# Taps right after their evacuation, weight splits ahead of it, and the residual scaled early: a reordered projection stage in a two-block fp32 kernel

## The chip, the cores and the metric

The program runs on one core of one Trainium2 chip. The metric is the device time of one execution in microseconds. The engines are TensorE (PE, the matrix multiplier), VectorE (DVE), ScalarE (ACT) and GpSimd (POOL); SyncE (SP), ACT and POOL also issue DMAs. Each engine works through its own instructions in order, and semaphores tie the engines together.

## The reference

Two transformer blocks on a sequence of 512 tokens with 1024 channels, in fp32. The first block (spatial gating, forgetting attention, a convolutional feed-forward net) is untouched by the change. Between the blocks stands a normalisation, and the second block starts from its result:

```python
    x = first_block(...)            # ends with: return rms_norm(x, norm_final_g)
    return second_block(x, ...)

def second_block(x, ...):
        h = rmsnorm(x, norm_gain[l])
        proj = jnp.einsum('btd,dc->btc', h, w_in[l])
        (dn_q, dn_k, dn_v, dn_z, dn_b, dn_a, df_q, df_k, df_v, df_z) = jnp.split(proj, ...)
        o_dn = gated_deltanet_group(...)
        o_df = diff_attention_group(...)
        x = x + jnp.einsum('btc,cd->btd', concat([o_dn, o_df]), w_out[l])

def gated_deltanet_group(q, k, v, z, bb, aa, conv_w, a_log, dt_bias, out_gain):
    qkv = silu(causal_depthwise_conv(concat([q, k, v]), conv_w))     # 4 taps
    q = l2norm(q) * DN_HEAD_K ** -0.5;  k = l2norm(k)
    beta = sigmoid(bb);  g = -exp(a_log) * softplus(aa + dt_bias)
    o = gated_delta_rule(q, k, v, g, beta)
    ...
```

## The kernel before

Activations lie channel-major in SBUF: X is 8 tiles (KC) of 128 channels x 512 tokens. Every fp32 product is made from three products of split numbers: a high part (GH for activations, HI for weights) and a low remainder (GL, LO). The function `product` makes one output tile of 128 channels from 8 x 3 matmuls of 128x512.

Weights arrive as a stream of units of 128x1024 in a ring of four slots. For each unit SP loads RAW and POOL loads HI (the same bytes, of which HI keeps the high part) as soon as `unit_done` says that the unit four places earlier is used up. DVE then makes LO = RAW - HI: that is `ring_low`, written as `("ring", unit)` in the order tables. A product waits for its unit's split (`unit_split`).

The stage in question is the first of the second block. It multiplies by the gates' unit (`ba`: beta and decay, 36 rows) and by twelve units `kqv` 0 to 11 (four tiles each of keys, queries, values of the delta rule, written to KT, QT, VT). For each tile t:

- PE makes the product in one of two banks (`bank_of`), and may start it when the tile two earlier has been evacuated (`gemm_freed`).
- DVE evacuates it times the token factor RB into CB (`evacuate`, L1509).
- ACT makes the last tap, CB times a weight (L1308).
- DVE adds three taps, each waiting for the one before it (L1894).
- ACT applies silu (L1315) and, for keys and queries, squares (L1320) into SQ2; PE sums the squares per token (`l2s`, L650). After four tiles ACT takes roots and DVE reciprocals (`l2r`), PE spreads them over the partitions (`l2b`, L656), and DVE multiplies (L1913).

Around these stand the gates' rows (`rows`: softplus, cumulative sums, exponentials, on ACT and DVE in turns), `lam` and `scalars` (the factor of differential attention), `egb` (rows reread from HBM), `cols` (the rows turned to columns), and `spill`, which writes X to HBM, as its place in SBUF is reused. At the kernel's end XR reads it back, DVE multiplies it by the final norm's gain and by R1B (the norm's token factor, spread over the partitions by PE into PS[6] and copied by ACT, L1312), and adds the last product.

After the twelve tiles PE goes on with `dfv` (values of differential attention), which waits for the evacuation of tile 11, and with `GK` 0, the Gram product of the keys, which waits for the last normalised key tile (`l2_made` 4, from `l2b` 3 on DVE).

What sets the order is written out by hand: all engines walk the same list, MIX2_ORDER, and each picks out what it has to do. `_projections` writes this stage's list and `_ring` puts the splits into it.

## Time and profile before

| | us |
|---|---|
| median of 3 runs | 984.22 (979.09 to 984.84) |
| the profiled execution | 979.09 |
| its span, first to last instruction | 977.4 |
| PE busy | 937.8 (96%) |
| DVE busy | 565.4 (58%) |
| ACT busy | 303.5 (31%) |
| mean granted clock of PE | 0.987 |

The time of the profiled execution is 1.7 us longer than its span, and it was the fastest of the three runs. PE is busy nearly throughout, so what counts is where it waits. The projection stage lies between about 590 and 677 us from the span's start.

### The profile page before, as it was taken

To read this page: it belongs to the slowest core of one execution; us is meant where nothing else is said; L and a number is where in the kernel's file an instruction comes from. 1 tells how busy PE (TensorE), PEld (TensorE's weight loads), DVE (VectorE), ACT (ScalarE), POOL (GpSimd) and SP (SyncE) were. 2 spreads that over 40 slices of the span, in tenths; PEclk is the share of its full clock that TensorE was granted. 3 is DMA by queue.
4 is the path that set the end of the run, shared out by engine and by line. 5 is a ranking of instruction groups with operands and counts; after the bars stand their busy time and mean duration, and the time that the engine had idled before them with its cause. 6 is when DMAs were issued, how large, how long until landed. Compare 5 with 4: busy or idle time off the path is not lost.

```text
span 977.4 us, 13547 instructions
## 1 busy us (share of the span) xinstructions
PE 937.8 (96%) x4666; PEld 762.6 (78%) x4666; DVE 565.4 (58%) x968; ACT 303.5 (31%) x609; POOL 72.3 (7%) x138
## 2 busy tenths in 40 slices
PE   9997998999999999999999999999999887889998
PEld 7886776788888888888888888888879774667777
DVE  6265446364877767776434336868563647625454
ACT  6143465433322222222101115434112234432410
POOL 0100000010110101010101000000000000000000
PEclk9998999999999999999999999999999989999999
DMA  8755332255656565656565655665353121113354
GB/s 275 228 187 193 129 130 88 87 177 179 204 185 202 183 203 183 204 181 205 179 205 178 200 186 166 218 210 166 105 161 120 45 86 44 44 44 108 110 187 156
DMA packets 49614, 154.84 MB, mean 158 GB/s; under 512 B 9488, under 2 KB 10512, under 8 KB 49312
## 3 DMA queue, kind: packets, MB, share of 16 engines
q1 hardware_dynamic: 22176, 75.70, 24.2%
q0 software_dynamic: 19008, 69.21, 21.7%
q10 hardware_dynamic: 8384, 9.29, 2.9%
q8 instruction: 31, 0.51, 0.2%
q14 instruction: 15, 0.12, 0.0%
HBM read 149.70 MB, written 4.49 MB: 158 GB/s over the span
## 4 chain that ended last, share of the span: by engine, by line
PE 85%; DVE 6%; ACT 3%; issue 3%; DMA 3%; ACTq 0%; DVEq 0%; SPq 0%; POOLq 0%
PE bank L593 70%; DMA HI<-wstream 2%; PE bank L650 2%; PE bank L1015 1%; PE bank L752 1%; PE bank L728 1%; PE bank L656 1%; PE bank L983 1%; PE bank L977 1%; PE bank L963 1%; PE bank L922 1%; PE bank L930 1%; PE bank L742 1%; DVE bank L1855 1%; PE bank L940 1%
## 5 line engine op out<-in xcount | busy, mean ns | idle before, releaser
L593 PE MATMUL bank<-GH,HI 128*128 128x512 f32 x720 | 290.1, 403 | 2.1 <-ACT DV L1355 1.4
L593 PE MATMUL bank<-GH,LO 128*128 128x512 f32 x720 | 282.4, 392 | 0.0
L593 PE MATMUL bank<-GL,HI 128*128 128x512 f32 x720 | 282.0, 392 | 0.0
L1517 DVE TENSOR_TENSOR LO<-RAW,HI 128x1024 fp32r<-128x1024 f32 x88 | 107.7, 1224 | 121.6 <-DMA HI<-wstream 120.7
L593 PEld LDWEIGHTS bank<-GH,HI 128*128 128x128 f32 x720 | 136.3, 189 | 31.3 <-issue 2.8
L593 PEld LDWEIGHTS bank<-GH,LO 128*128 128x128 f32 x720 | 135.9, 189 | 29.1
L593 PEld LDWEIGHTS bank<-GL,HI 128*128 128x128 f32 x720 | 136.3, 189 | 25.4
L575 POOL DMA_DIRECT2D HI<-wstream x132 | 69.8, 529 | 880.5 <-PE bank L593 871.5
L1238 ACT ACTIVATE YC<-AB,PAR 128x512 f32<-128x512 f32 x44 | 36.0, 818 | 140.5 <-DVE AB L1664 140.5
L593 PE MATMUL bank<-AH,HI 128*128 128x512 f32 x176 | 69.4, 394 | 0.0
L593 PE MATMUL bank<-AH,LO 128*128 128x512 f32 x176 | 69.0, 392 | 0.0
L593 PE MATMUL bank<-AL,HI 128*128 128x512 f32 x176 | 68.4, 388 | 0.0
L1664 DVE TENSOR_TENSOR AB<-bank,RB 128x512 f32<-128x512 f32 x44 | 30.4, 691 | 48.5 <-PE bank L593 48.5
L1658 DVE TENSOR_TENSOR LO<-RAW,HI 128x1024 fp32r<-128x1024 f32 x44 | 53.6, 1219 | 3.6 <-DMA HI<-wstream 3.6
L593 PEld LDWEIGHTS bank<-AH,LO 128*128 128x128 f32 x176 | 33.0, 188 | 7.7
L593 PE MATMUL bank<-HI,GH 128*128 128x512 f32 x96 | 38.4, 400 | 0.5 <-DVE LO L1524 0.5
L593 PEld LDWEIGHTS bank<-AL,HI 128*128 128x128 f32 x176 | 33.0, 188 | 7.3
L1126 ACT ACTIVATE GH<-X,SM 128x512 fp32r<-128x512 f32 x8 | 5.8, 725 | 104.7 <-DVE X L1722 104.7
L593 PEld LDWEIGHTS bank<-AH,HI 128*128 128x128 f32 x176 | 33.1, 188 | 6.6
L593 PE MATMUL bank<-LO,GH 128*128 128x512 f32 x96 | 37.5, 390 | 0.0
L593 PE MATMUL bank<-HI,GL 128*128 128x512 f32 x96 | 37.4, 390 | 0.0
L1675 DVE SCALAR_TENSOR_TENSOR YC<-AB,PAR,YC 128x512 f32<-128x512 f32 x44 | 33.1, 752 | 6.0 <-DVE YC L1671 0.3
(289 smaller groups left out, 1264.0 us busy)
## 6 DMA issues: line engine op xcount, KB each, us to landing
RAW<-wstream SPq DMA_DIRECT2D x135, 512.0 KB, 3.8
HI<-wstream POOLq DMA_DIRECT2D x132, 512.0 KB, 4.9
X<-x_t SPq DMA_DIRECT2D x8, 256.0 KB, 7.7
NCB<-out_t ACTq DMA_DIRECT2D x1, 2048.0 KB, 10.2
out_t<-X ACTq DMA_DIRECT2D x8, 256.0 KB, 5.2
XR<-out_t ACTq DMA_DIRECT2D x8, 256.0 KB, 3.6
out_t<-XR SPq DMA_DIRECT2D x8, 256.0 KB, 2.6
EG<-out_t ACTq DMA_DIRECT2D x1, 1024.0 KB, 4.9
```

The costliest lines, as they stand in the source:

```text
L575: pool.dma_start(HI[:, s, :], wstream[bass.ds(2 * i + s // 2, 1), :, 1024 * (s % 2):1024 * (s % 2 + 1)] .rearrange("o p n -> p (o n)")).th ...
L593: mm = pe.matmul(out, a, b, start=(first and n == 0), stop=(last and n == 2))
L650: mm = pe.matmul(out[:, n * b:n * (b + 1)], src[:, P * b:P * (b + 1)], groups, start=True, stop=True)
L656: mm = pe.matmul(out[:, P * b:P * (b + 1)], column(b), IDENT, start=True, stop=True)
L728: pe.matmul(PS[2 + e][:, 0:w], q[r, 4 + p, P * i:P * (i + 1)], k[r, p, 0:w], start=(part == 0), stop=False)
L742: mm = pe.transpose(PS[4 + e][:, P * j:P * (j + 1)], P1[:, 2 * (n % 2) + e, P * j:P * (j + 1)], IDENT)
L752: mm = pe.matmul(PS[6][64 * e:64 * e + 64, P * j:T], VB[:, j, P * p + 64 * e:P * p + 64 * (e + 1)], PT1[:, e, j, P * j:T], start=(j == 0), ...
L1238: act.activation(YC[:, gv, :], AB[:, gv, 2:T + 2], ACT.Identity, scale=PAR[:, bass.ds(6 * t + (C_FCW + 3 * gv + 2), 1)], bias=PAR[:, bass. ...
L1517: dve.tensor_tensor(LO[:, u % RING, :], RAW[:, u % RING, :], HI[:, u % RING, :].bitcast(F32), ALU.subtract).then_inc(unit_split, 1)
L1658: dve.tensor_tensor(LO[:, slot, :], RAW[:, slot, :], HI[:, slot, :].bitcast(F32), ALU.subtract).then_inc(unit_split, 1)
L1664: dve.tensor_tensor(AB[:, gv, 2:T + 2], up_bank(G_UP + 2 * tt + gv)[:, :], RB[:, :], ALU.mult)\
L1675: dve.scalar_tensor_tensor(YC[:, gv, :], AB[:, gv, 0:T], PAR[:, bass.ds(6 * t + (C_FCW + 3 * gv), 1)], YC[:, gv, :], ALU.mult, ALU.add).th ...
```

## The change

The change has five parts. (1) Each tile's taps, silu and square come right after its evacuation in the list, instead of behind the other work of its round. (2) The split of the unit three ahead (`ring`) comes before the evacuation of a tile, not after it. (3) The gates' rows, `egb`, `scalars` and `cols` are moved later, behind tiles whose taps are now complete. (4) X is multiplied by gain and token factor in place, straight from PS[6], in four steps (`x2`, 8 DVE instructions) behind tiles 7 to 10, and is written to HBM after that; so R1B, ACT's copy into it and the 8 multiplications at the kernel's end go, and `dfv` 0 waits for the eight updates. (5) In the first round PE makes tile 0's products with k = 2 to 6 before the last product of the gates' unit. Besides, the sums of squares of tiles 4 to 7 go to the same bank as those of 0 to 3.

```diff
 def _projections():
-    order = [("ba", 0), ("rows", 0)]
+    order = [("ba", 0)]
     for t in range(12):
         if t in (6, 10):
             order.append(("l2r", t // 4 - 1))
         order.append(("kqv", t))
+        if t == 5:
+            order.append(("scalars", 0))
+        if t in (0, 2):
+            order.append(("rows", t // 2))
         if t == 0:
-            order += [("lam", 0), ("rows", 1)]
-        if t == 2:
+            order.append(("lam", 0))
+        if t == 4:
             order.append(("egb", 0))
-        if t == 3:
-            order.append(("scalars", 0))
-        if t == 5:
+        if 7 <= t <= 10:
+            order.append(("x2", t - 7))
+        if t == 6:
             order.append(("cols", 0))
-        if 4 <= t <= 7:
-            order.append(("spill", t - 4))
         if 2 <= t <= 9:
             order.append(("l2s", t - 2))
         if t >= 8:
             order.append(("l2b", t - 8))
-        order.append(("taps", t))
...
 def _ring(order):
     for what, n in order:
+        if what == "kqv" and n:
+            out.append(("ring", U_KQV + n + RING - 1))
         out.append((what, n))
-        if what == "kqv":
-            out.append(("ring", U_KQV + n + RING - 1))
...
+        elif what == "ba":
+            out.append(("ring", U_KQV + RING - 1))
...
             def head_sums(t):
                 pe.wait_ge(l2_sq, t + 1)
-                token_sums(PS[5 + 2 * (t // 4)][:, NB * t:NB * (t + 1)], SQ2[:, t % 2, :]).then_inc(l2_mm, 1)
+                if t == 4:
+                    pe.wait_ge(l2_rt, 1)
+                token_sums(PS[5][:, NB * t:NB * (t + 1)], SQ2[:, t % 2, :]).then_inc(l2_mm, 1)
...
+                    product(U_KQV, G_KQV, gl_made, 2 * KC, ks=range(2, KC - 1))
                     product(U_BA, G_BA, gl_made, 2 * KC, ks=(KC - 1,))
-                    product(U_KQV, G_KQV, gl_made, 2 * KC, ks=range(2, KC))
+                    product(U_KQV, G_KQV, gl_made, 2 * KC, ks=(KC - 1,))
...
                     if n == 0:
                         pe.wait_ge(gemm_freed, G_DFQK)
                         pe.wait_ge(rb_ready, 3)
-                        pe.wait_ge(r1_kept, 1)
+                        pe.wait_ge(x_updated, KC)
...
                     act.activation(tile_of(n), CB[:, n % 2, 3:T + 3], ACT.Copy,
                                    scale=par(C_DCW + 4 * n + 3)).then_inc(cv_a, 1)
-                    if n == 0:
-                        act.wait_ge(r1_mm, 1)
-                        act.activation(R1B[:, :], PS[6][:, :], ACT.Copy).then_inc(r1_kept, 1)
-                elif what == "taps":
                     act.wait_ge(cv_v, n + 1)
                     act.activation(tile_of(n), tile_of(n), ACT.Silu).then_inc(cv_s, 1)
...
-                elif what == "spill":
+                elif what == "x2":
                     if n == 0:
                         act.wait_ge(scratch_landed, LANDED_ROWS)
                     for k in (2 * n, 2 * n + 1):
                         if k < KC - 1:
+                            act.wait_ge(x_updated, k + 1)
                             act.dma_start(out_t[P * k:P * (k + 1), :], X[:, k, :]).then_inc(x_spilled, 16)
...
                 elif what == "kqv":
                     evacuate(G_KQV + n, U_KQV + n, CB[:, n % 2, 3:T + 3])
-                elif what == "taps":
                     dve.wait_ge(cv_a, n + 1)
...
+                elif what == "x2":
+                    dve.wait_ge(r1_mm, 1)
+                    for k in (2 * n, 2 * n + 1):
+                        dve.scalar_tensor_tensor(X[:, k, :], X[:, k, :], par(C_GFIN + k), PS[6][:, :],
+                                                 ALU.mult, ALU.mult).then_inc(x_updated, 1)
...
             for m in range(KC):
                 dve.wait_ge(x_landed[m], 32)
-                then(dve.scalar_tensor_tensor(XR[:, m, :], XR[:, m, :], par(C_GFIN + m), R1B[:, :], ALU.mult, ALU.mult))
                 dve.wait_ge(unit_done, U_WO2 + m + 1)
```

Two engines show how the order moves. DVE at the start of the stage, from the evacuation of the gates' product (BR) on; CB is the evacuated tile, LO the split, KT the taps, R_.. and RS the gates' rows. Before:

```order
L1509 TENSOR_TENSOR BR<-bank,RB 36x512
L1886 MEMSET CB 128x2x3
L1748 TENSOR_SCALAR R_99<-BR,PAR 4x512
L1749 MEMSET RS 128x512
L1509 TENSOR_TENSOR CB<-bank,RB 128x512
L1517 TENSOR_TENSOR LO<-RAW,HI 128x1024
L1753 TENSOR_SCALAR R_99<-R_99 4x512
L1754 TENSOR_TENSOR R_99<-R_99,R_100 4x512
L1755 TENSOR_SCALAR R_99<-R_99,SM 4x512
L1757 SCALAR_TENSOR_TENSOR RS<-CON,R_99 4x64 x8
L1762 TENSOR_TENSOR R_99<-RS 4x512
L1894 SCALAR_TENSOR_TENSOR KT<-CB,PAR,KT 128x512 x3
```

Now, in the changed kernel (its own line numbers):

```order
L1513 TENSOR_TENSOR BR<-bank,RB 36x512
L1890 MEMSET CB 128x2x3
L1521 TENSOR_TENSOR LO<-RAW,HI 128x1024
L1513 TENSOR_TENSOR CB<-bank,RB 128x512
L1897 SCALAR_TENSOR_TENSOR KT<-CB,PAR,KT 128x512 x3
L1752 TENSOR_SCALAR R_98<-BR,PAR 4x512
L1753 MEMSET RS 128x512
L1521 TENSOR_TENSOR LO<-RAW,HI 128x1024
L1513 TENSOR_TENSOR CB<-bank,RB 128x512
L1897 SCALAR_TENSOR_TENSOR KT<-CB,PAR,KT 128x512 x3
```

The split moved ahead of the evacuation, and the taps follow it at once; the rows' sums (L1753 to L1762 before) moved behind tile 2.

ACT at the same place, from its copy of the token factor RB on. Before:

```order
L1274 ACTIVATE RB<-bank 128x512
L1280 ACT_TABLE_LOAD
L1280 ACTIVATE SM<-PAR 4x1
L1282 ACTIVATE R_100<-R_99 4x512
L1284 ACTIVATE R_100<-R_100 4x512
L1286 ACT_TABLE_LOAD
L1286 ACTIVATE R_100<-R_100,SM 4x512
L1308 ACTIVATE KT<-CB,PAR 128x512
L1312 ACTIVATE R1B<-bank 128x512
L1303 ACT_TABLE_LOAD
L1303 ACTIVATE SM<-bank 128x2
```

Now:

```order
L1279 ACTIVATE RB<-bank 128x512
L1313 ACTIVATE KT<-CB,PAR 128x512
L1316 ACT_TABLE_LOAD
L1316 ACTIVATE KT<-KT 128x512
L1321 ACTIVATE SQ_101<-KT 128x512
L1285 ACT_TABLE_LOAD
L1285 ACTIVATE SM<-PAR 4x1
L1287 ACTIVATE R_99<-R_98 4x512
L1289 ACTIVATE R_99<-R_99 4x512
L1291 ACT_TABLE_LOAD
L1291 ACTIVATE R_99<-R_99,SM 4x512
L1308 ACT_TABLE_LOAD
L1308 ACTIVATE SM<-bank 128x2
L1313 ACTIVATE KT<-CB,PAR 128x512
```

The gates' softplus (L1280 to L1286 before) and the exponential of `lam` (L1303 before), with their three table loads, moved from ahead of tile 0's copy to between tile 0's square and tile 1's copy.

## Rows read from the trace of the kernel before

**Rows 1.** Page, part 4: the chain that ended last, by engine
```profile
PE 85%; DVE 6%; ACT 3%; issue 3%; DMA 3%; ACTq 0%; DVEq 0%; SPq 0%; POOLq 0%
```

**Rows 2.** Windows: busy us of PE, PEld, DVE, ACT, POOL; granted clock; DMA
```profile
590.00:700.00 110.00, 109.05 (x585) 93.44 (x584) 76.71 (x120) 44.30 (x61) 8.44 (x16) 1.00 0.56 177
```

**Rows 3.** Timeline of PE: start us, us, instruction, [idle before it, releaser]
```profile
612.81 1.05 PE L650 MATMUL bank<-CON,SQ 128*128 128x1 f32 x8 [0.68 <-ACT SQ L1320]
...
676.22 1.05 PE L886 MATMUL bank<-KT 128*128 128x128 f32 x8
```

**Rows 4.** Timeline of DVE, first tile: split, rows, taps, next evacuation
```profile
602.62 1.23 DVE L1517 TENSOR_TENSOR LO<-RAW,HI 128x1024 fp32r<-128x1024 f32 x1
604.89 0.42 DVE L1753 TENSOR_SCALAR R<-R 4x512 f32<-4x512 f32 x1 [1.05 <-ACT R L1286]
...
608.76 2.30 DVE L1894 SCALAR_TENSOR_TENSOR KT<-CB,PAR,KT 128x512 f32<-128x512 f32 x3
```

**Rows 5.** Timeline of ACT, same stretch
```profile
600.09 1.28 ACT L1280 ACT_TABLE_LOAD   x1
...
602.85 1.28 ACT L1286 ACT_TABLE_LOAD   x1
...
604.77 0.70 ACT L1308 ACTIVATE KT<-CB,PAR 128x512 f32<-128x512 f32 x1
...
607.26 0.17 ACT L1303 ACTIVATE SM<-bank 128x2 f32<-128x2 f32 x1
...
612.13 0.63 ACT L1320 ACTIVATE SQ<-KT 128x512 f32<-128x512 f32 x1
```

**Rows 6.** Timeline of DVE, tile 8: evacuation, split, normalisation, taps
```profile
651.69 0.69 DVE L1509 TENSOR_TENSOR CB<-bank,RB 128x512 f32<-128x512 f32 x1 [2.15 <-PE bank L593]
652.42 1.23 DVE L1517 TENSOR_TENSOR LO<-RAW,HI 128x1024 fp32r<-128x1024 f32 x1
653.56 0.68 DVE L1913 TENSOR_TENSOR KT<-KT,bank 128x512 f32<-128x512 f32 x1
654.16 2.33 DVE L1894 SCALAR_TENSOR_TENSOR VT<-CB,PAR,VT 128x512 f32<-128x512 f32 x3
```

**Rows 7.** Timeline of ACT, tile 8: the copy
```profile
652.42 0.72 ACT L1308 ACTIVATE VT<-CB,PAR 128x512 f32<-128x512 f32 x1 [1.55 <-DVE CB L1509]
```

**Rows 8.** Timeline of DVE: cols, the reciprocal of l2r, two multiplies from a bank
```profile
634.20 0.48 DVE L1901 MEMSET ST<- 128x512 f32 x1
...
635.38 2.32 DVE L1894 SCALAR_TENSOR_TENSOR QT<-CB,PAR,QT 128x512 f32<-128x512 f32 x3
...
640.65 0.25 DVE L1910 RECIPROCAL SM<-SM 128x16 f32<-128x16 f32 x1 [2.94 <-ACT SM L1360]
...
934.02 1.40 DVE L1974 SCALAR_TENSOR_TENSOR QT<-bank,PAR,ZT 128x512 f32<-128x512 f32 x2
```

**Rows 9.** The chain in order of time: start us, us, engine, line, count
```profile
613.86 5.61 PE bank L593 x24
```

**Rows 10.** HI loads: one issue on POOL, and time to landing, 585 to 680
```profile
595.07 0.53 POOL L575 DMA_DIRECT2D HI<-wstream  x1 [8.13 <-PE bank L593]
...
DMA to landing us min/median/max: 4.5/5.4/6.3
```

**Rows 11.** Windows around three waits of PE: columns as in rows 2
```profile
84.00:90.00 6.00, 0.85 (x5) 0.39 (x3) 5.50 (x14) 2.49 (x5) 0.00 (x0) 0.94 0.36 116
90.00:96.00 6.00, 6.00 (x19) 4.81 (x20) 1.04 (x5) 2.43 (x10) 0.00 (x0) 0.50 0.00 0
...
724.00:727.00 3.00, 1.33 (x11) 0.92 (x9) 0.00 (x0) 0.63 (x1) 0.54 (x1) 1.00 0.88 198
727.00:731.00 4.00, 4.00 (x26) 3.49 (x24) 2.48 (x6) 1.09 (x2) 0.00 (x0) 1.00 0.26 93
```

**Rows 12.** Timeline of DVE at the kernel's end
```profile
969.42 0.75 DVE L1989 SCALAR_TENSOR_TENSOR XR<-XR,PAR,R1B 128x512 f32<-128x512 f32 x1
974.26 0.69 DVE L1991 TENSOR_TENSOR XR<-XR,bank 128x512 f32<-128x512 f32 x1 [4.09 <-PE bank L593]
```

8 lines of the change are left out of this document (4 added, 4 removed).

## The prediction, made before the changed kernel ran

> **What bounds the kernel now.** I read the chain that ended last first: PE holds 85% of it [rows 1], so a change can only pay, or cost, where PE waits. Then the windows of the projection stage: of 110 us PE is busy 109.05, DVE 76.71 and ACT 44.30, at a granted clock of 1.00 [rows 2]. So 0.95 us is all that any reordering can win there. The timeline of PE shows 0.68 of it as one wait, for the squares of tile 0 [rows 3]. DVE looks free for a third of the time, but the sums say nothing about how its waits are spread: the reader should see in the timelines of DVE and ACT what stands between one tile's taps and the next one's, and how it was hidden. Before the change, DVE used the time of ACT's copy for a split (evacuation 651.69, split 652.42, taps 654.16; ACT's copy of 0.72 ran beside the split) [rows 6, 7], and the rows' softplus on ACT ran beside the product and the split of tile 0, before any tap was due [rows 4, 5].
>
> **The change, part by part.** The marker is the start of Gram product 0, which in the trace begins at 676.22 [rows 3]. It needs the last normalised key tile, which is last in DVE's order of this stage, so it shows when DVE and ACT are through. I follow their chain in the new order.
>
> Start of the chain. The split of unit `kqv` 3 now stands ahead of the evacuation of tile 0. Its load may start when the gates' unit is used up, and that is now 15 matmuls later. A tile's 24 matmuls take 5.6 us [rows 9], so these are 3.4 to 3.5. The load's issue goes from 595.07 to about 598.5, and it lands 5.4 (median) to 6.3 us later [rows 10]: 603.9 to 604.8. The next load is issued under 1 us behind it, so I take 604.2. Before, the same split ran at 602.62 without a wait [rows 4]. DVE waits some 3 us here with nothing else to do, and the evacuation, the copy and everything after stand behind it.
>
> One round of DVE. Split 1.14 (652.42 to 653.56), evacuation 0.73 (651.69 to 652.42), ACT's copy 0.72 plus a step of 0.03, three taps 2.25 (2.33 less the overlap with the next instruction) [rows 6, 7]. Together 4.87. The copy's 0.75 is new on this path: the split that hid it stands before the evacuation now. Tile 0's taps end at 604.2 + 4.87 = 609.1.
>
> The detour on ACT. ACT now does tile 0's silu and square (0.63 each), then the softplus and `lam`, then tile 1's copy. From the rows: one table load and three activations 2.76 (600.09 to 602.85), a load and the logarithm 1.92 (to 604.77), a load of 1.28 with the exponential of 0.17, the copy 0.70 [rows 5]. With the two of 0.63 that is 8.1 us, in which DVE's taps of tile 1 wait: until 617.2. They end at 619.4. This is the work that used to be hidden, and its cover is gone because a tile's taps now stand on both sides of it.
>
> The rest. Ten more rounds (tiles 2 to 11) are 48.7. Between them stand on DVE: the rows' sums 3.87 (604.89 to 608.76) [rows 4]; `cols` 1.18; `x2` 8 instructions at 1.40 a pair, 5.6 [rows 8]; four multiplications of `l2b` at 0.60, 2.4 [rows 6]; `l2r` 0, for which DVE waits until ACT has done silu, square, a table load and the root, 0.63 + 0.63 + 1.28 + 0.3, and then 0.2 for itself, 3.1; `l2r` 1 the same but with `x2` and `l2b` beside it (2.0 us), while ACT also waits for the updates and issues two writes of X, some 1.7. Sum 17.8. The chain ends at 619.4 + 48.7 + 17.8 = 685.9, against 676.22: **9.7 us later**. With the landing at 603.8 it is 9.3, at 604.8 it is 10.3.
>
> Is PE ahead of it all the time? Yes by its own pace: a tile is 5.6 us [rows 9] and the sums about 0.8 between (1.05 with its overlap) [rows 3], so after 0.68 us less at tile 0 PE would reach Gram product 0 at 675.3. It is then held where its waits look: by the squares of tile 1 (619.4 + 1.3 = 620.7, wanted at 618.5), 2 us; by the evacuation of tile 3, before tile 5, 2 us; by the first roots, 3 us, a wait that is new at the sums of tile 4, since both groups share a bank; by the evacuation of tile 11 before `dfv` 0, about 2 us, since its split and the last `x2` and `l2b` now stand ahead of it; and by the last key tile, 1 us. These are 10 us. The eight updates of X are done before tile 11's evacuation and hold nothing by themselves. The loads on SP and POOL follow `unit_done`, so they shift with PE, and have at least 0.5 us to spare against DVE after the first one, except near tile 7, where a landing of 6.3 instead of 5.4 would add 0.5.
>
> After the stage. The next chain (decays, Gram products, their gather and scatter through HBM) starts from PE's and DVE's last steps here, and so moves as a whole; I see nothing that gives time back. At the end of the kernel 8 instructions of 0.75 go, but DVE waits 4.09 us for PE behind the last of them [rows 12]: 0 us.
>
> The clock. A wait of about 5 us (84 to 90) was followed by six microseconds at 0.50, which is 1.2 GHz; one of 1.67 us (724 to 727) by 1.00 throughout [rows 11]. New waits of 2 to 3 us lie between. A fall costs half of its length in matmuls where PE sets the time. I count one, at the 3 us wait before tile 7: it bounds from 0 to 3 us, and I take 1.7, since the wait is nearer to the row of 1.67 than to that of 5.
>
> **Sum:** 9.7 + 1.7 = 11.4 us. On the profiled execution of 979.09 (span 977.4 and 1.7 around it) that is 990.5; on the median of 984.22 it is 995.6. The measured median should lie between, nearer to the second, as two of three runs lie near 984: **995**.
>
> ACT's table loads bear most on the detour. In the rows a load takes 1.28 and the whole step with the logarithm 1.92 [rows 5], 0.64 more, which is what an activation of this size takes (0.63): nothing else is paid for the switch. The Trainium skill, "ScalarE: Activation LUTs", section "What ACT_TABLE_LOAD costs", puts a drain of about 1380 ns beside a load of about 1283 ns; the load agrees with the trace, the drain does not show in it. By that page the five loads on the path would add an estimated 6.9 us more, and the sum would be 18.3.
>
> **The rivals.**
> 1. *The stage stays PE-bound.* If DVE, busy for 76.71 of 110 us, kept up, only the 0.95 us of idle would go: 984.2 - 0.9 = 983.3. For it speaks the sum of busy times [rows 2]; against it that twelve rounds of 4.87, 17.8 of inserts and the 8.1 us detour fill the stage without a gap. 0.12.
> 2. *Only the late waits hold.* The detour is absorbed and PE waits only before `dfv` 0 and Gram product 0, where the split stands ahead of tile 11's evacuation: 3 us less the 0.95: 986.3. It needs the first landing before 601 and a detour under 3 us; neither fits the rows. 0.11.
> 3. *The clock falls after three or four waits.* The waits at tiles 1, 5, 6 and before `dfv` 0 each cost up to 1.7, partly absorbed by the next wait: 9.7 + 5 = 14.7, or 998.9. The row of 0.50 speaks for it, the one of 1.67 us against. 0.12.
> 4. *The end was bound by DVE.* The 8 multiplications at 0.75 were on the path in the last 30 us: 6.0 and the 0.95 go, 977.3, faster than before. It decides if DVE is never waiting for PE there; the 4.09 us of waiting says that it is. 0.03.
> 5. *Each switch of tables costs its drain too*, as if ACT stood still after every load. Priced by the rows, as one more load of 1.28 at each of the five on the path [rows 5], it adds 6.4: 984.2 + 17.8 = 1002.0. The rows speak against it, since the logarithm is through 0.64 us after its load. This is the rule of the Trainium skill's page above, whose own figure gives 1002.5. 0.03.
>
> **How the numbers follow.** My forecast, 9 to 13 us more, has 0.59; the rivals have 0.12, 0.11, 0.12, 0.03 and 0.03. The range runs from the profiled execution's 979.09 plus 9.3 without a fall of the clock, 988.4, to 999 with the third rival; I put the lower end at 987.5. That leaves out rivals 1, 2, 4, 5 for the most part, some 0.2 to 0.25, and it is as wide as the unknown base (979 or 984) and the clock make it. One per cent, 9.8 us, is about what a measurement of this kernel can tell from no change. My bare chain of 9.3 to 10.3 lies on that line, and the clock pushes over it: four in five of the forecast, and rivals 3 and 5, are slower by more, 0.60; rivals 1 and 2 and the rest of the forecast are within, 0.36; faster 0.04.
>
> **What the next profile would show.** DVE waiting some 3 us for the HI load of the first split, near 601; taps of tile 1 starting near 617, not 613; DVE nearly without waits for PE until 685; PE waiting five times, on ACT's squares, on DVE's evacuations and on ACT's root, 10 us in all; Gram product 0 near 686; the tail's DVE rows shorter and the tail itself as long as before. The prediction is wrong if tile 1's copy on ACT comes before 614, if PE's waits sum to under 5 us, or if the distance from Gram product 0 to the end is not the 301 us that it was.

## The result, and the profile of the changed kernel

| | before | changed |
|---|---|---|
| median, us | 983.24 (979.09 to 984.84, 4 runs) | 993.37 (992.38 to 994.17, 4 runs) |
| ratio, 95% interval | | 1.0135, 1.0093 to 1.0177 |
| profiled execution, its span | 979.09, 977.4 | 996.08, 994.4 |
| end of ACT's copy of RB | 600.08 | 602.83 |
| start of Gram product 0 | 676.22 | 692.78 |
| from the first to the second: the stage | 76.14 | 89.95 |
| Gram product 0 to the end of the span | 301.18 | 301.62 |

The changed kernel is slower, by 9 to 17 us. The medians are those of four executions each; the ratio comes from more: 24 executions of the changed kernel, and from the experiments 70 of the kernel before, are on record. Their means are 995.9 and 983.3, 12.6 apart, give or take 1.7. (One execution of the kernel before and one of a_ba, over 1.5% above the fastest of their kernel, are left out of all means and ratios.)

In the profiled pair the spans differ by 17.0: 2.75 arose ahead of the stage, in code whose work the change doesn't touch, 13.8 in the stage, 0.4 behind it. The stage is measured from ACT's copy of the token factor RB, since nothing of it can be evacuated earlier; that takes the 2.75 out. Each stage below is that of one profiled execution. How much it varies between executions of one kernel is not on record, so what follows from a stage is held against the times of all executions further down.

PE's share of the chain that ended last, from part 4 of the page, answers to [rows 1]. DVE has taken most of what PE lost (6 to 10%); ACT, the DMAs and "issue" have one per cent more each:

```profile
PE 76%; DVE 10%; issue 4%; ACT 4%; DMA 4%; ACTq 0%; DVEq 0%; SPq 0%; POOLq 0%
```

The windows of the changed kernel, with the columns of [rows 2]. The first row is the same stretch of 110 us: PE is now idle for almost 10 us of it, and its mean clock is 0.95, not 1.00. The other two show where the clock was at 0.50, one of its two levels (1.2 GHz), for all or a part of the row:

```profile
590.00:700.00 110.00, 100.33 (x492) 83.97 (x491) 74.64 (x120) 47.49 (x64) 7.38 (x14) 0.95 0.50 166
625.00:630.00 5.00, 4.08 (x14) 3.60 (x15) 4.04 (x7) 2.06 (x4) 0.00 (x0) 0.50 0.45 163
651.00:655.00 4.00, 3.87 (x16) 3.27 (x17) 3.00 (x5) 1.93 (x2) 0.00 (x0) 0.67 0.44 155
```

What PE waited for in the stage of the changed kernel (waits: us in total, times, longest), 9.7 us. Before there were 0.95, of which 0.68 was one wait [rows 3]:

```profile
PE bank L652 <- ACT SQ L1321: 3.0, 1, 3.0
PE bank L652 <- ACT SM L1363: 2.7, 1, 2.7
PE bank L595 <- DVE CB L1513: 1.5, 1, 1.5
PE bank L595 <- DVE LO L1521: 1.4, 1, 1.4
PE bank L890 <- DVE KT L1922: 0.8, 1, 0.8
PE bank L595 <- issue: 0.3, 1, 0.3
```

They are, in this order, the squares of tile 1, the first roots, the evacuation of tile 11 ahead of `dfv` 0, the evacuation of tile 0 ahead of tile 2 (it ends right after DVE's split, which the profile names), and the last key tile ahead of Gram product 0. The sixth, 0.3, was there before.

The chain that ended last, in order of time, at the start of the stage. Each row is the piece that the next one had waited for, so it can be read as a list of what sets the time (a load on POOL's queue, the split, the evacuation of tile 0, ACT's copy, three taps, silu, square, then a detour over ACT, the copy of tile 1 and its taps):

```profile
601.26 7.59 DMA HI<-wstream
...
608.93 1.22 DVE LO L1521
610.15 0.61 DVE CB L1513
610.79 0.73 ACT KT L1313
...
611.62 0.76 DVE KT L1897
...
613.98 0.65 ACT KT L1316
614.64 0.64 ACT SQ L1321
615.29 1.28 ACT L1285
...
617.99 1.28 ACT L1291
619.29 0.72 ACT R L1291
620.03 1.28 ACT L1308
621.32 0.17 ACT SM L1308
621.50 0.62 ACT KT L1313
...
622.21 0.76 DVE KT L1897
```

Before, the split ran at 602.62 without a wait. The softplus with its two loads ran beside the evacuation and the split, all but the last 1.05 us, for which DVE waited, and `lam`'s load ran beside the rows' sums [rows 4, 5]. The timeline of DVE in the changed kernel shows the two big waits, 5.19 for the load and 5.67 for ACT's copy of tile 1, and then the round in which nothing hides the copy (0.86 between evacuation and taps, every time). From 635.91 to 640.83 and from there to 645.75 a bare round takes 4.92:

```profile
608.93 1.22 DVE L1521 TENSOR_TENSOR LO<-RAW,HI 128x1024 fp32r<-128x1024 f32 x1 [5.19 <-DMA HI<-wstream]
611.62 2.33 DVE L1897 SCALAR_TENSOR_TENSOR KT<-CB,PAR,KT 128x512 f32<-128x512 f32 x3 [0.86 <-ACT KT L1313]
622.21 2.33 DVE L1897 SCALAR_TENSOR_TENSOR KT<-CB,PAR,KT 128x512 f32<-128x512 f32 x3 [5.67 <-ACT KT L1313]
...
635.91 2.33 DVE L1897 SCALAR_TENSOR_TENSOR KT<-CB,PAR,KT 128x512 f32<-128x512 f32 x3 [0.86 <-ACT KT L1313]
640.83 2.33 DVE L1897 SCALAR_TENSOR_TENSOR QT<-CB,PAR,QT 128x512 f32<-128x512 f32 x3 [0.86 <-ACT QT L1313]
645.75 2.33 DVE L1897 SCALAR_TENSOR_TENSOR QT<-CB,PAR,QT 128x512 f32<-128x512 f32 x3 [0.86 <-ACT QT L1313]
...
659.39 0.69 DVE L1513 TENSOR_TENSOR CB<-bank,RB 128x512 f32<-128x512 f32 x1 [0.71 <-PE bank L595]
```

Between the taps of tile 1 and Gram product 0 that last row is the longest of DVE's waits for PE; a wait of 0.24 for a load at 664.82 is the only other one that is neither for the copy nor for the roots. The chain of DVE and ACT is the bound here although DVE is busy for only 63 of 90 us.

**PE's account.** PE does the same work in this stage in every kernel, so its length must be a constant, plus PE's waits, plus what the low clock took. The last is summed from windows of 2 us, each length times (1 less the granted clock). This was done for all 14 kernels of this study (names as below):

| kernel | stage | waits of PE | lost to the clock | stage less both | ratio to before (95%) |
|---|---|---|---|---|---|
| before | 76.14 | 1.0 | 0.0 | 75.1 | |
| changed | 89.95 | 9.7 | 5.1 | 75.1 | 1.0135 (1.0093 to 1.0177) |
| u_ba: part 5 undone | 83.49 | 6.5 | 1.7 | 75.3 | 1.0092 (1.0043 to 1.0140) |
| u_ring: part 2 undone | 83.34 | 4.6 | 3.4 | 75.3 | 1.0112 (1.0045 to 1.0178) |
| u_rows: `rows` 0 moved back | 90.02 | 9.7 | 5.1 | 75.2 | 1.0137 (1.0078 to 1.0197) |
| u_bank: second bank back | 89.95 | 10.2 | 5.1 | 74.7 | 1.0164 (1.0104 to 1.0224) |
| u_x2: part 4 undone | 88.89 | 8.1 | 5.1 | 75.7 | 1.0122 (1.0079 to 1.0166) |
| u_taps: parts 1 and 2 undone | 84.71 | 6.0 | 3.4 | 75.3 | 1.0059 (1.0022 to 1.0095) |
| u_ba_ring: parts 2 and 5 undone | 82.87 | 4.5 | 3.4 | 75.0 | 1.0030 (1.0000 to 1.0061) |
| a_ba: part 5 alone | 81.12 | 2.8 | 3.4 | 74.9 | 1.0033 (1.0002 to 1.0064) |
| a_ring: part 2 alone | 80.88 | 2.5 | 3.4 | 75.0 | 1.0001 (0.9975 to 1.0027) |
| a_ba_ring: parts 2 and 5 alone | 84.98 | 6.7 | 3.4 | 74.9 | 1.0088 (1.0057 to 1.0119) |
| b_taps: taps ahead of the inserts alone | 76.34 | 1.4 | 0.0 | 74.9 | 0.9985 (0.9951 to 1.0019) |
| b_x2: part 4 alone | 77.01 | 1.8 | 0.0 | 75.2 | 1.0003 (0.9967 to 1.0039) |

The remainder is 75.1 within 0.6 us in all fourteen rows. So in each profiled execution the stage is explained in full from PE's side; what is left to explain is what makes PE wait, and what the clock does in the other executions.

**The times of all executions.** The second question can be put to the record, since each execution has its mean granted clock. The executions of the kernel before had 0.976 to 0.992, and their times run from 976.4 to 991.7, the longer ones mostly at the lower clock. One thousandth of 980 us is 0.98 us. Below is how much longer the mean execution is than that of the kernel before, measured beside it (for the changed kernel: all 70), with bounds of two standard errors; the new PE waits from the table above; and what the difference of the mean granted clocks makes over the whole execution:

| kernel | mean time over before | new waits of PE in the stage | by the mean clock | sum of both |
|---|---|---|---|---|
| changed | 12.6 ± 1.7 | 8.8 | 3.0 | 11.7 |
| u_ba | 8.7 ± 4.0 | 5.5 | 2.0 | 7.5 |
| u_ring | 8.6 ± 3.9 | 3.6 | 5.2 | 8.8 |
| u_rows | 10.8 ± 2.9 | 8.8 | 0.8 | 9.5 |
| u_bank | 14.9 ± 3.6 | 9.2 | 8.2 | 17.4 |
| u_x2 | 13.6 ± 3.3 | 7.1 | 3.4 | 10.6 |
| u_taps | 5.6 ± 2.6 | 5.0 | 0.2 | 5.2 |
| u_ba_ring | 2.8 ± 2.1 | 3.5 | -0.2 | 3.4 |
| a_ba | 3.4 ± 2.5 | 1.8 | 0.8 | 2.6 |
| a_ring | 0.5 ± 2.0 | 1.6 | -2.1 | -0.6 |
| a_ba_ring | 9.4 ± 2.6 | 5.8 | 3.2 | 9.0 |
| b_taps | -0.3 ± 2.6 | 0.4 | -0.6 | -0.1 |
| b_x2 | 2.3 ± 2.7 | 0.9 | 1.6 | 2.4 |

The sum meets the measured difference within about 3 us in every row. So the waits count in the times as they do in the stage. Whether a kernel's lower mean clock comes of its waits or of chance these runs don't settle. What the clock took in the stage of one trace doesn't carry over: a_ring lost 3.4 us there and its ten executions have a higher mean clock than the kernel before (0.987 against 0.985), and in the traces of b_taps and b_x2, whose stages lost nothing, the low clock took 20.5 and 20.8 us over the whole span, against 12.3 in that of the kernel before (summed from the same windows of 2 us).

### The profile page after: what moved, and what is told of

Read it like the earlier page. It is cut to its first block, busy times and chain, and to the rows that moved or that the text cites. A ratio compares the mean times of both kernels' runs of the same rounds, so it can differ in the third digit from the quotient of the medians.

```text
span 994.4 us, 13564 instructions
## 1 busy us (share of the span) xinstructions
PE 941.9 (95%) x4666; PEld 763.8 (77%) x4666; DVE 564.1 (57%) x968; ACT 307.1 (31%) x611; POOL 72.4 (7%) x138
## 4 chain that ended last, share of the span: by engine, by line
PE 76%; DVE 10%; issue 4%; ACT 4%; DMA 4%; ACTq 0%; DVEq 0%; SPq 0%; POOLq 0%
PE bank L595 63%; DMA HI<-wstream 3%; DVE LO L1521 2%; PE bank L652 1%; PE bank L754 1%; PE bank L1019 1%; PE bank L730 1%; PE bank L987 1%; PE bank L981 1%; PE bank L967 1%; PE bank L926 1%; PE bank L744 1%; PE bank L934 1%; DVE KT L1897 1%; PE bank L944 1%
## 5 line engine op out<-in xcount | busy, mean ns | idle before, releaser
L595 PE MATMUL bank<-AL,HI 128*128 128x512 f32 x176 | 68.3, 388 | 0.0
```

The costliest lines, as they stand in the source:

```text
L595: mm = pe.matmul(out, a, b, start=(first and n == 0), stop=(last and n == 2))
```

## The experiments

Three views were held against each other. *Serial chain*: DVE and ACT form one chain through the stage, and its length, with the late first load at its head, sets the time. *Single waits*: each PE wait is a cost of its own and goes with the part that causes it. *Landing by chance*: the first load landed late in that one execution. The first four kernels each undo one part of the changed kernel.

**u_ba: part 5 undone**

```diff
-                    product(U_KQV, G_KQV, gl_made, 2 * KC, ks=range(2, KC - 1))
                     product(U_BA, G_BA, gl_made, 2 * KC, ks=(KC - 1,))
-                    product(U_KQV, G_KQV, gl_made, 2 * KC, ks=(KC - 1,))
+                    product(U_KQV, G_KQV, gl_made, 2 * KC, ks=range(2, KC))
```

> The changed kernel with part 5 alone undone: PE makes the last product of the gates' unit before tile 0's products with k = 2 to 7, as before. The measure is the stage: from the end of ACT's copy of RB to the start of Gram product 0, 76.1 us in the kernel before and 90.0 us in the changed one. Serial chain of DVE and ACT (my theory): the load of the first split is issued 3.4 us earlier and is no longer issued right behind its neighbour, so DVE's wait of 5.2 us for it nearly goes and everything behind it moves up: stage 85 to 86, time 4 to 5 us under the changed kernel. Rival, single waits of PE: only PE's 1.4 us wait before tile 2 goes, stage 88.5, and the later waits stay as they are. Rival, the landing of 7.6 to 8.0 us was chance: stage 87 to 88 with the changed kernel's order in other runs too.

The stage fell from 89.95 to 83.49. The two HI loads are issued 4.1 us apart again, and the view of POOL's HI tile gives 4.7 to 5.2 us to landing; the split starts without a wait. In DVE's timeline of u_ba the detour of 5.67 is untouched, and evacuation and taps stand 5.2 us earlier, counted from RB's end (601.19):

```profile
603.28 0.68 DVE L1512 TENSOR_TENSOR CB<-bank,RB 128x512 f32<-128x512 f32 x1
604.83 2.33 DVE L1896 SCALAR_TENSOR_TENSOR KT<-CB,PAR,KT 128x512 f32<-128x512 f32 x3 [0.86 <-ACT KT L1312]
...
615.42 2.33 DVE L1896 SCALAR_TENSOR_TENSOR KT<-CB,PAR,KT 128x512 f32<-128x512 f32 x3 [5.67 <-ACT KT L1312]
```

The taps of tile 1 start 14.2 us after it instead of 19.4. These 5.2 us are the late issue and landing; the other 1.3 of the 6.5 arose further on. Of the 1.3, 0.95 are DVE's two small waits at 659.39 and 664.82 in the changed kernel, which u_ba doesn't have. The result is below both forecasts, 85 to 86 for the chain and 88.5 for single waits, but nearer to the chain, and the start of tile 1's taps is what it asks for. Chance falls with the runs together: in all eight kernels that have part 5 the two loads took 7.0 to 8.8 us, in the six that haven't it 4.5 to 5.6.

**u_ring: part 2 undone.** The split stands between evacuation and taps, and hides ACT's copy.

```diff
-        if what == "kqv" and n:
-            out.append(("ring", U_KQV + n + RING - 1))
...
-        elif what == "ba":
-            out.append(("ring", U_KQV + RING - 1))
...
                     evacuate(G_KQV + n, U_KQV + n, CB[:, n % 2, 3:T + 3])
+                    ring_low(U_KQV + n + RING - 1)
                     dve.wait_ge(cv_a, n + 1)
```

> The changed kernel with part 2 alone undone: each tile's split stands between its evacuation and its taps again. Serial chain: ACT's copy (0.86 us of DVE waiting for each of twelve tiles) is hidden by the split again, 12 x 0.86 = 10.3 us at most, of which two are under the detour and the first load anyway: stage 81 to 83, time 7 to 9 under the changed kernel. Single waits: only the wait of 1.5 us before dfv 0 and that of 0.8 at Gram product 0 go: stage 87.7.

83.34, just over the 81 to 83 of the chain and far from the 87.7 of single waits. The load lands as late as in the changed kernel (7.30 us after its issue), but tile 0's evacuation and copy are done by then, and each later round is shorter. DVE waits for PE at the evacuations of tiles 5, 7, 8 and 9 (0.72 to 1.16 us each): PE sets the pace there, until the second roots put DVE behind again (PE waits 1.0 for the last key tile). The time shows less than the stage: 7 to 9 us under the changed kernel were expected, the means are 4.0 apart. In the profiled execution the low clock took 11.9 us behind the stage, against 5.5 in the changed kernel's.

**u_rows: `rows` 0 ahead of tile 0 again**, as before the change.

```diff
-    order = [("ba", 0)]
+    order = [("ba", 0), ("rows", 0)]
...
-        if t in (0, 2):
-            order.append(("rows", t // 2))
+        if t == 2:
+            order.append(("rows", 1))
```

> The changed kernel with one piece of part 3 undone: the gates' softplus (rows 0) stands before tile 0 in the list again, lam and everything else as changed. Serial chain: two table loads and four activations (615.3 to 620.0 in the changed kernel's trace, 4.7 us) leave the stretch between tile 0's square and tile 1's copy and run while DVE waits for its first load: stage 85 to 86, time 4 to 5 under the changed kernel. Single waits: PE's 3.0 us at the sums of tile 1 goes and so does the fall of the clock behind it, stage 85.5 too; so this run tells the cause of the first wait, not the two theories apart, except that in the chain the later waits of PE (2.7 at the sums of tile 4, 1.5 before dfv 0) shrink as well.

A miss: 90.02, nothing won, where both views had about 85.5. DVE's timeline of u_rows shows why. The split still holds the rows' first operation on DVE, and so ACT's softplus stands now between that and the copy of tile 0. The detour was divided, 2.99 ahead of tile 0's taps and 1.79 ahead of tile 1's, against 0.86 and 5.67, with the first table load out of the way, beside DVE's wait for its load; but that load landed 8.41 us after its issue, not 7.59, and two operations of the rows were added ahead of the evacuation:

```profile
614.13 2.32 DVE L1897 SCALAR_TENSOR_TENSOR KT<-CB,PAR,KT 128x512 f32<-128x512 f32 x3 [2.99 <-ACT KT L1313]
...
619.99 2.33 DVE L1897 SCALAR_TENSOR_TENSOR KT<-CB,PAR,KT 128x512 f32<-128x512 f32 x3 [1.79 <-ACT KT L1313]
```

Their start from RB's end is 18.45 against 19.38. This 0.9 was lost again further on, 0.7 of it behind the last taps: PE had waited 1.91 us for the evacuation of tile 11 and then came late to Gram product 0 by itself, at a granted clock of 0.66 in the last 5 us. Moving the softplus ahead does nothing as long as it hangs on the same late load.

**u_bank: the sums of tiles 4 to 7 in a bank of their own again**, so that PE need not wait for the roots.

```diff
-                if t == 4:
-                    pe.wait_ge(l2_rt, 1)
-                token_sums(PS[5][:, NB * t:NB * (t + 1)], SQ2[:, t % 2, :]).then_inc(l2_mm, 1)
+                token_sums(PS[5 + 2 * (t // 4)][:, NB * t:NB * (t + 1)], SQ2[:, t % 2, :]).then_inc(l2_mm, 1)
...
-                                   PS[5][:, 16 * n:16 * n + 16].rearrange("p (t b) -> p t b", b=NB), ACT.Sqrt,
+                                   PS[5 + 2 * n][:, 16 * n:16 * n + 16].rearrange("p (t b) -> p t b", b=NB), ACT.Sqrt,
```

> The changed kernel with the sums of squares of tiles 4 to 7 in a bank of their own again, so that PE need not wait for ACT's first roots (2.7 us, followed by a stretch at half clock). Serial chain: DVE itself waits for the same roots (2.7 us before its reciprocal) and is behind PE everywhere, so the stage stays at 90, at most 1 us less for the clock. Single waits: 2.7 and the clock's 1.7 go, stage 85.6, time 4 under the changed kernel.

This decides between chain and single waits. The wait for the roots (2.7 us) is gone and the stage is 89.95, the same to the last digit. In the timeline of PE in u_bank the time reappears ahead of `dfv` 0, at 5.52 instead of 1.53:

```profile
686.21 0.80 PE L595 MATMUL bank<-HI,GH 128*128 128x512 f32 x1 [5.52 <-DVE CB L1511]
```

A wait of PE is only the place at which PE notices that the chain is late. (That the digits are the same is chance: the waits are 0.5 longer and the remainder 0.5 shorter.)

**u_x2: part 4 undone.** The copy of R1B is back on ACT, the multiplications at the tail.

```diff
-                elif what == "x2":
-                    dve.wait_ge(r1_mm, 1)
-                    for k in (2 * n, 2 * n + 1):
-                        dve.scalar_tensor_tensor(X[:, k, :], X[:, k, :], par(C_GFIN + k), PS[6][:, :],
-                                                 ALU.mult, ALU.mult).then_inc(x_updated, 1)
...
+                then(dve.scalar_tensor_tensor(XR[:, m, :], XR[:, m, :], par(C_GFIN + m), R1B[:, :], ALU.mult, ALU.mult))
```

> The changed kernel with part 4 alone undone: the copy R1B is back on ACT (now where the first write of X stands, ahead of tile 7's inserts), the writes of X wait for nothing on DVE, and the eight multiplications are back at the tail. Serial chain of DVE and ACT: eight instructions of 0.70 us leave the chain behind tile 7, so the stage (end of ACT's copy of RB to Gram product 0) shrinks by 5.6 us, from 89.95 to about 84.4, unless PE's own pace takes over, which at 76 us plus some 5 us of waits at tiles 1 to 6 sets a floor near 82. The wait before dfv 0 (1.5 us) and before Gram product 0 (0.8 us) goes. Gram product 0 to the end stays at 301 apart from transfers that land late. Single waits of PE: only those two waits go, 2.3 us, stage 87.6. Landing was chance: no change of the stage beyond a landing's 2 us.

Another miss of the chain, taken as a bare sum: 88.89, not 84.4. 0.6 us of it is a later landing (8.20). The rest shows in DVE's timeline behind tile 7. Without the updates DVE is early there, and waits for the next unit's load, 1.25 and 1.07 us instead of 0.24 and nothing, and 0.9 us longer for the second roots:

```profile
665.93 1.23 DVE L1522 TENSOR_TENSOR LO<-RAW,HI 128x1024 fp32r<-128x1024 f32 x1 [1.25 <-DMA HI<-wstream]
...
672.68 1.22 DVE L1522 TENSOR_TENSOR LO<-RAW,HI 128x1024 fp32r<-128x1024 f32 x1 [1.07 <-DMA HI<-wstream]
...
681.18 0.25 DVE L1914 RECIPROCAL SM<-SM 128x16 f32<-128x16 f32 x1 [2.31 <-ACT SM L1365]
```

From the taps of tile 6 to those of tile 11 the changed kernel takes 35.92 us and u_x2 34.24: of 5.6 us of work, 1.7 were on the path. With sums, spreading and product PE needs some 7 us a tile there (7.26 between the evacuations of tiles 8 and 9 in the kernel before), as much as DVE with the updates, and a load is issued only when PE is through with a unit. So the chain has a second limit close beside it, through `unit_done` and the load; this follows from the code and these rows, and no run varied it.

**u_taps: split behind the evacuation, taps and silu behind the inserts.** By the numbers in *The change* these are parts 2 and 1; the expectation calls them 2 and 3. What stays is the order of the inserts (3), the updates of X and part 5.

```diff
+        order.append(("taps", t))
...
-        if what == "kqv" and n:
+        out.append((what, n))
+        if what == "kqv":
             out.append(("ring", U_KQV + n + RING - 1))
-        out.append((what, n))
...
-        elif what == "ba":
-            out.append(("ring", U_KQV + RING - 1))
...
+                elif what == "taps":
                     dve.wait_ge(cv_a, n + 1)
```

> The changed kernel with parts 2 and 3 undone together: a tile's split stands behind its evacuation again, and its taps and silu behind the inserts of its turn. Parts 1, 4 and 5 stay. Serial chain of DVE and ACT: a round is evacuation 0.73, split 1.14 beside ACT's copy, taps 2.25, so 4.12 instead of 4.87 us, under PE's 5.6. The softplus still stands between the copy of tile 0 and that of tile 1, so taps of tile 1 wait once for it, by some 4 to 5 us instead of 5.7. After that DVE gains 1.5 us a tile and PE sets the pace: stage 79 to 81, with PE's waits in the first 30 us and 1 to 2 us at the roots. Single waits of PE: the late waits and that at tile 1 stay at 5 us, stage 85 or more. Landing was chance: stage as in the changed kernel, 88 to 90.

84.71, where 79 to 81 was expected. The taps of tile 1 wait 3.58 instead of 5.67, as the chain has it, but PE waits 2.84 for the squares of tile 1 and then runs at 0.50, which costs 3.4 and was not in the estimate. Undoing part 1 on top of part 2 brought nothing over u_ring's 83.34 in the stage.

The next two are the kernel before with one thing added.

**b_taps: taps and silu ahead of the inserts, alone**

```diff
         order.append(("kqv", t))
+        order.append(("taps", t))
...
-        order.append(("taps", t))
     return order
```

> The kernel before with one thing alone: a tile's taps and silu stand directly behind its split, ahead of the inserts of its turn (the split stays between evacuation and taps, the rows' softplus ahead of tile 0). Serial chain of DVE and ACT: the round stays at 4.12 us, since the split still hides ACT's copy. The inserts, among them the rows' sums and the logarithm's table load on ACT behind tile 0, now stand between two tiles' taps, and each has 1.5 us of slack a tile against PE. I expect one PE wait of 0 to 3 us near tile 1, 1 to 2 us at the roots (the root's reciprocal stands right behind silu and square of tile 5 on ACT), stage 76 to 80 against 76.14 of the kernel before, time within 0.4%. Single waits of PE: as much. If taps behind the evacuation were by themselves what costs 10 us, the stage would be 86 or more.

76.34, ratio 0.9985: nothing lost. PE's waits in b_taps, with the clock at 1.00 throughout:

```profile
PE bank L886 <- DVE KT L1913: 1.1, 1, 1.1
PE bank L593 <- issue: 0.3, 1, 0.3
```

The wait for tile 0's squares, 0.68 before [rows 3], is gone, and 1.1 appears ahead of Gram product 0. Taps directly behind the evacuation are harmless where a split stands between them and the softplus ahead of both.

**b_x2: part 4 alone**

```diff
-        if 4 <= t <= 7:
-            order.append(("spill", t - 4))
+        if 7 <= t <= 10:
+            order.append(("x2", t - 7))
```

(with `x2`, the waits for `x_updated` and the tail as in the change.)

> The kernel before with part 4 alone: X is updated on DVE with eight instructions behind tiles 7 to 10, R1B and its copy on ACT go, and so do the eight multiplications at the tail. Serial chain of DVE and ACT: DVE has 76.71 of 110 us and rounds of 4.12 us against PE's 5.6 to 6.4, so each pair of 1.40 fits the slack of its tile; behind tile 10, with the second roots and a multiplication beside it, 1 to 2 us may be left over. Stage 76.1 to 78, Gram product 0 to the end 301 as before, time within 0.3% of before: what costs in the changed kernel costs nothing where DVE has slack. Single waits of PE: stage up to 78. A tail bound by DVE: 6 us less behind Gram product 0, so 295.

77.01 and 1.0003. DVE is busy for 62.56 us of this stage, 5 more than before, at no cost that can be measured, and the tail without its eight multiplications gives nothing back: Gram product 0 to the end is 306.73 in this execution, of which the low clock took 12.3, and without that it is 294.4 against 294.0 before (301.18 less 7.2).

That leaves parts 5 and 2. The revised theory was a *conjunction*: the late load costs only where evacuation, copy and taps stand behind its split.

**a_ba: part 5 alone**

```diff
+                    product(U_KQV, G_KQV, gl_made, 2 * KC, ks=range(2, KC - 1))
                     product(U_BA, G_BA, gl_made, 2 * KC, ks=(KC - 1,))
-                    product(U_KQV, G_KQV, gl_made, 2 * KC, ks=range(2, KC))
+                    product(U_KQV, G_KQV, gl_made, 2 * KC, ks=(KC - 1,))
```

> The kernel before with part 5 alone: the gates' last three matmuls stand 15 matmuls later, so the load of the kqv 3 split is issued 3.4 us later and 0.9 us ahead of the next one. Conjunction (the revised theory: the late landing costs only because evacuation, copy and taps stand behind the split that waits for it, in a chain without slack): the split starts 5.9 to 6.9 us after ACT's copy of RB, as in the changed kernel, but evacuation 0 and ACT's copies are done by then. Taps 0 end near 12 us after RB instead of 11.2; PE waits 0 to 2 us for the squares of tile 0 or the evacuation of tile 1, then DVE catches up. Stage 76.1 to 78.5, time within 0.4% of before. Late landing alone: stage 82 or more, since 6.5 us were won where this part was undone.

**a_ring: part 2 alone**

```diff
+        if what == "kqv" and n:
+            out.append(("ring", U_KQV + n + RING - 1))
         out.append((what, n))
-        if what == "kqv":
-            out.append(("ring", U_KQV + n + RING - 1))
...
+        elif what == "ba":
+            out.append(("ring", U_KQV + RING - 1))
```

> The kernel before with part 2 alone: each split stands ahead of its tile's evacuation; the first load is issued as early as before, so that split starts some 2 us after RB without a wait. Conjunction: a round is 4.87 us where the inserts don't hide ACT's copy and 4.12 where they do, both under PE's 5.6; stage 76.1 to 78, time within 0.4% of before. Exposed copy: the 0.75 us a tile is the loss by itself, 11 x 0.75 = 8 us, stage 82 or more.

Both stages missed in the same way, 81.12 and 80.88 where 76 to 78.5 and 76 to 78 were expected, while both times, within 0.4% of the kernel before, came out as expected. PE waits once in each, for the squares of tile 0; the timeline of PE in a_ba, then in a_ring:

```profile
615.49 1.57 PE L650 MATMUL bank<-CON,SQ 128*128 128x1 f32 x8 [2.50 <-ACT SQ L1321]
```

```profile
615.31 1.36 PE L652 MATMUL bank<-CON,SQ 128*128 128x1 f32 x8 [1.88 <-ACT SQ L1322]
```

The size of these waits is exact to follow. The taps of tile 0 start 8.68 us after RB's end before the change (608.76 less 600.08, [rows 4]), 10.50 in a_ba and 9.89 in a_ring. The delays are 1.82 and 1.21; the waits grew from 0.68 to 2.50 and to 1.88, by 1.82 and 1.20. So the chain split, rows, softplus, rows' sums, taps, silu, square of tile 0 had no slack in the kernel before: its 0.68 us of waiting was the end of it. In a_ring the split delays the rows' first operation and through it ACT's softplus, which waits 1.08 us for it. In these two traces the larger part comes behind the wait: a fall of the clock. Windows of a_ba:

```profile
616.00:618.00 2.00, 2.00 (x8) 1.81 (x9) 1.85 (x3) 0.05 (x1) 0.00 (x0) 0.50 0.89 311
618.00:620.00 2.00, 2.00 (x6) 1.57 (x5) 1.97 (x3) 1.53 (x3) 0.00 (x0) 0.50 0.01 4
620.00:622.00 2.00, 2.00 (x6) 1.56 (x5) 1.81 (x4) 0.35 (x1) 0.00 (x0) 0.50 0.74 201
```

PE is busy in full and does half as much; DVE, which has slack, then waits for PE (2.68 us at the evacuation at 625.39), so here the 3.4 us are added in full. 1.8 + 3.4 makes up the 5.0 of a_ba, within the 0.2 of the remainder. In the times the loss is smaller, 0.0 to 0.6% for a_ba and none that can be told for a_ring (1.0001). The clock accounts for the gap: the profiled execution of a_ring, 987.98, is the slowest of its ten, and over all executions its mean clock was no lower than that of the kernel before. The waits of 1.8 and 1.6 us are what these two parts cost by themselves; the 3.4 us are what that one execution lost in that place.

**a_ba_ring: both on the kernel before** (the two diffs above together)

> The kernel before with parts 2 and 5 together. Conjunction: the split waits for its landing until 6 us after RB and the rows' first operations, evacuation 0, ACT's softplus and the copy of tile 0 stand behind it; taps 0 start near 12 to 14 us after RB (10.7 in the kernel before: 610.76 less 600.08 would be 10.7; in the changed kernel 8.8), behind the rows' sums of 3.9 us. The rounds are under PE's pace, so part of the delay is taken back: stage 79 to 84, time 0.3 to 0.9% over before, while either part alone stays under 78.5. Single parts: no more than the sum of both alone.

84.98, just over the 79 to 84 that was expected, ratio 1.0088. PE waits 4.5 us for the squares and 2.2 before. The two together cost 8.8 us of stage, little short of the sum of both alone, 9.7, so the stage doesn't single out the conjunction. By waits alone it is 5.8 (6.7 less 0.95) against 1.85 + 1.55 = 3.4 for the two alone: the waits do more than add up, and one fall of the clock in each of the three traces hides it. The mean times show an excess too, 9.4 us against 3.4 + 0.5, but with bounds of about 4 on it, and by the table above more of it is the clock (4.5) than the waits (2.4).

**u_ba_ring: both undone in the changed kernel** (the diffs of u_ba and u_ring together)

> The changed kernel with parts 2 and 5 undone together (each alone brought the stage from 89.95 to 83.4). Conjunction: either one removes the same thing, the late landing ahead of evacuation, copy and taps, so both together bring little more than one: the softplus between the copies of tiles 0 and 1 stays in the chain (5.5 us), the rounds are 4.12. Stage 79 to 82, against 77 if their gains of 6.5 us add up. Time 0.3 to 0.8% over before.

82.87, where each alone gave 83.4. In the stage the gains of 6.5 us don't add up, and in the waits neither (3.2 and 5.1 alone, 5.2 together), as if either removed the same thing. The times can't confirm it: 3.9 and 4.0 us are won by each alone and 9.8 by both, with bounds of 2 to 4 on each. What stays in the chain is the detour; DVE's timeline of u_ba_ring:

```profile
604.07 2.32 DVE L1893 SCALAR_TENSOR_TENSOR KT<-CB,PAR,KT 128x512 f32<-128x512 f32 x3
...
614.58 2.33 DVE L1893 SCALAR_TENSOR_TENSOR KT<-CB,PAR,KT 128x512 f32<-128x512 f32 x3 [4.73 <-ACT KT L1308]
```

By now DVE has enough slack to take the 4.73 back before PE needs it; PE waits 3.1 us for the first roots instead and 1.1 at the end, and the clock falls after the first (3.4 us). What this kernel still has of the change costs 2.8 us in the mean time, give or take 2.1. With a bank of its own for tiles 4 to 7 the wait for the roots should go; that was not run.

## Why the prediction was right

The measured median of 993.37 lies 1.6 us under the 995 of the prediction, in its range, on the side that had 0.60. The mechanism held in its steps; three sizes were off: the landing, the fall of the clock and, a little, the base.

- *The kernel before.* One reading was off. The prediction has the softplus run before any tap was due, but tile 0's taps stood behind the rows' sums, and these behind 1.05 us of waiting for ACT [rows 4]; a_ba and a_ring show that this chain had no slack. It doesn't enter the sum.
- *Start of the chain.* The issue was right: 1.57 us before RB's end, where 595.07 + 3.4 gives 1.6. The landing was not: it took 7.59 us, and the prediction took 5.7, from rows in which loads are 4 us or more apart [rows 10]. This is the largest miss within the chain, 2.0 us: the split starts 6.1 us after RB's end and not 4.1. "Some 3 us" of waiting were 5.19.
- *One round of DVE.* 4.87 predicted, 4.92 measured. The copy's 0.75 was 0.86 from end to start.
- *The detour.* 8.1 predicted. From 613.98 (silu of tile 0) to 622.21 it took 8.2, with each piece as in the sum.
- *The rest.* From the end of tile 1's taps to that of the last multiplication 66.5 predicted, 68.3 measured: 0.5 from the rounds, 0.95 from one wait each for PE and a load, which the sum had not, and 0.3 in small pieces.
- *PE's waits.* Ten predicted, 9.7 measured, at four of the five places: 3.0 for tile 1 (2 predicted), 2.7 for the roots (3), 1.5 ahead of `dfv` 0 (2), 0.8 at the last key tile (1). The one "before tile 5" didn't come; 1.4 came instead ahead of tile 2, for tile 0's evacuation, which the late landing had held.
- *The clock.* The mis-sized term: one fall and 1.7 us predicted, 5.1 measured in the stage of this execution. (Over all executions the changed kernel's mean granted clock is 0.982 against 0.985, worth 3.0 us.) The way in which it was added was wrong too. Where DVE sets the pace, a slower PE only fills time in which it would have waited; in DVE's chain it shows as 0.71 us. Where PE sets the pace, as in a_ba behind its wait, it is added in full. From PE's side the account is 8.75 of new waits + 5.1 = 13.8; from DVE's side it is the predicted 9.7, + 2.0 landing, + 1.8 in the rest, + 0.3 up to tile 1's taps. These are two accounts of the same 13.8 us, not to be summed.
- *After the stage.* 301 predicted, 301.62 against 301.18. That the tail's eight multiplications were worth nothing holds; DVE's last two waits for PE, 4.09 before where one followed a multiplication [rows 12], are 4.75 each without them.
- *The base.* The stage lost 13.8 in one pair of executions, the medians of four 10.1, and the means of all executions 12.6, against 11.4 predicted. New waits of 8.8 and a clock worth 3.0 make 11.7 of these: the sum's two terms, 9.7 and 1.7, are near both, and the clock's being so near over the mean is luck, since nothing in the prediction said how often it falls.

The rivals: the first (PE-bound) and the second (late waits only) fall with the waits above; the fourth with the tail. The third, several falls of the clock, came true in the profiled execution, with two falls at 0.50 that took 5.1 us, but it had them on top of the chain, at 998.9; the mean of all executions is 995.9. The fifth falls: in ACT's timeline of the changed kernel an activation starts 0.01 to 0.02 us behind each of these two loads,

```profile
617.99 1.28 ACT L1291 ACT_TABLE_LOAD   x1
619.29 0.72 ACT L1291 ACTIVATE R<-R,SM 4x512 f32<-4x512 f32 x1
620.03 1.28 ACT L1308 ACT_TABLE_LOAD   x1
621.32 0.17 ACT L1308 ACTIVATE SM<-bank 128x2 f32<-128x2 f32 x1
```

and a load starts 0.02 us behind the activation before it. The Trainium skill, "ScalarE: Activation LUTs", section "What ACT_TABLE_LOAD costs", has about 1380 ns of drain beside the load; no row here shows any.

Which part costs, then. Parts 1 and 4 cost nothing that can be told by themselves (b_taps, b_x2), and giving the second bank back wins nothing (u_bank). Parts 5 and 2 add 1.8 and 1.6 us of waits to the kernel before, by delaying tile 0 by 1.8 and 1.2 us in a chain without slack, and both together 5.8; in mean time they cost 3.4, 0.5 and 9.4. In the changed kernel undoing either wins 6.5 us of stage and some 4 of time, undoing both 7.1 and 9.8. What is left in u_ba_ring, 6.7 us of stage of which the low clock has 3.4, and 2.8 of time, belongs to the softplus between the copies of tiles 0 and 1 and the roots that PE must now wait for. How it divides between the two is open. No kernel beat the one before; b_taps is equal to it within 0.5%.

## What to carry to other kernels

A stage that is 99% busy on PE can hide a second engine's chain that has no slack at all: before moving a step, follow the first tile from its load to the place where PE uses its result, and count what is added ahead of it there, not the busy shares. When a wait is removed and the time stays, look for the next place where the same engine waits (u_bank). Account for the time from the bound engine's side as constant work plus waits plus lost clock; if the remainder is constant over all variants, nothing is missing in those traces. Then hold it against the times: one trace shows one course of the clock, and here it stood for the others in the waits but not in what the clock took.
